# Router scaling and gate split moved to the third chunk, with the first loads cut smaller, in a two-layer streaming encoder

## The chip, the cores and the metric

The kernel runs on one core of one Trainium2 chip. The metric is the device time of one execution in microseconds (us), as the median of several runs.

## The reference, cut to what matters

Two layers over 256 tokens of width 2048. Layer 0 mixes the tokens with stick-breaking attention (16 heads), layer 1 with an mLSTM (8 heads); behind each mixer stands a mixture of 32 experts of which each token uses two.

```python
def reference(x, norm_mix, norm_ffn, norm_final, sb_w_in, sb_w_out, ml_w_in, ...):
    for i in range(DEPTH):
        h = rmsnorm(x, norm_mix[i])
        if i % N_MIXERS == 0:
            x = x + stick_breaking_mixer(h, sb_w_in[j], sb_w_out[j])   # qkv = h @ w_in: 2048 x 6144
        else:
            x = x + mlstm_mixer(h, ml_w_in[j], ml_b_i[j], ml_b_f[j], ml_g_head[j], ml_w_out[j])
        h = rmsnorm(x, norm_ffn[i])
        x = x + hierarchical_moe(h, moe_w_group[i], ..., moe_w1[i], moe_w3[i], moe_w2[i])
    return rmsnorm(x, norm_final)
```

What the change touches is the start of layer 0: `h @ w_in` for the first four heads, and the small tensors that are needed later, the router's weights (`moe_w_group`, `moe_w_expert`, 2048 x 36), its biases, the mLSTM's gate columns of `ml_w_in` (2048 x 16) and biases.

## The kernel before, in words

**Weights come in slots of 1 MB.** The projection of a layer runs in four groups of heads; a group has three chunks of 512 columns (queries, keys, values in layer 0), and a chunk four slots, each 512 rows of the weight by 512 columns. SyncE's queue loads a slot into one of three places (`raw_loaded`), ScalarE rounds it into a high part (`split_hi`, L417, semaphore `hi_made`), VectorE subtracts to get the low part (`split_lo`, L421, `lo_made`), and TensorE multiplies each of them with the high and low parts of the transposed x (`project`, 48 products of 256 columns for a slot of chunks 0 and 1, 24 of 512 for one of chunk 2). All of `lo_made`'s counts are in slot order: TensorE waits for slot j with `lo_made >= j + 1`, and the queue loads slot j once `lo_made` is j - 2. Places of both parts are three as well, so ScalarE can be at most three slots ahead of TensorE.

**The order on ScalarE and VectorE is written out.** `schedule` makes a list of steps with a position in eighths of a slot: the split of slot j stands at position 8(j - 2), the evacuation of the three chunks (`take_chunk` on VectorE, `take_values` on ScalarE) at 32, 64 and 96, just behind the split of slots 6, 10 and, for the last, 13 (slots 12 and 13 are the next group's first two). Each engine walks the list in order, and whatever it waits for holds all behind it. In the first group of layer 0, the step of chunk 0 also has these, in L1528 and L1576 to L1583 on VectorE and L1340 on ScalarE:

```python
if kind == "first" and k == 0:
    scale_router(layer)          # waits small_loaded, multiplies router_w by the norm's scale
...
if kind == "first" and k == 0:
    split_gates(act)             # waits small_loaded[0], rounds gate_w into gate_hi
```

`small_loaded[0]` counts all twenty small loads that GpSimd issues one behind the other (`load_small`, L610 to L615, then L668 to L673): six of router weights, two of biases, eight of gate columns, four more. GpSimd also splits slot 1 of each layer (`split_lo_one`, L640) before it issues them, and masks the attention scores of all groups behind them (`keep_causal`, L646).

**The start.** SyncE loads three scale rows, x in two pieces of 1 MB (128 tokens each), and slots 0, 1 and 2. TensorE turns x (`turn_x`, L713) into eight PSUM banks' worth of tiles, "units" u of two k-tiles; for each ScalarE writes the scaled high part (L1222) and VectorE the low part (L1482). Between them ScalarE splits slot 0 (behind u = 1) and slot 1 (behind u = 3), and VectorE slot 0's low part (behind u = 1). Slots 1 and 2 of `lo_made`: the low part of slot 1 comes from GpSimd, and VectorE adds that count itself behind its eight units.

After the four groups come the output projection, the router, and the experts, whose weights SyncE streams while TensorE works.

## Time and profile before

| what | before |
|---|---|
| median of 3 runs (lowest to highest) | 1791.12 us (1789.12 to 1791.99) |
| the profiled execution: its time, its span | 1790.06 us, 1788.3 us |
| busy: TensorE, VectorE, ScalarE, GpSimd | 1561.9 (87%), 728.8 (41%), 423.0 (24%), 63.2 us (4%) |
| mean granted TensorE clock | 0.944 |
| read from memory | 540.83 MB, 304 GB/s over the span |
| chain that ended last, by engine | PE 48%, issue 29%, DMA 14%, SP's queue 3%, others 2% or less each |

The page shows the busy tenths of TensorE in 40 slices of 44.7 us: `7599999999997887788699999999999887888775`. The second slice, 44.7 to 89.4 us, is the emptiest of all but the last; the granted clock has its lowest digit there as well (`9799...`).

### The profile page before, as it was taken

What the parts mean: (1) busy time and instruction counts of PE and PEld (TensorE: products, weight loads), DVE (VectorE), ACT (ScalarE), POOL (GpSimd) and SP (SyncE); (2) the same over time, 40 slices, a digit from 0 to 9 for tenths busy, and PEclk for the clock granted to TensorE, in tenths of its full rate; (3) what the DMA queues carried; (4) which work ended last, traced back from release to release, by engine and by line L of the source; (5) the groups of instructions that cost most, each with busy time, mean ns of one, the idle gap of its engine ahead of it and who ended that gap; (6) DMA issues with size and microseconds to landing.
All of it is one profiled execution on the core that took longest, in us unless ns stands there. A gap on an engine that the chain in (4) does not pass through costs nothing.

```text
span 1788.3 us, 25607 instructions
## 1 busy us (share of the span) xinstructions
PE 1561.9 (87%) x9901; PEld 1066.0 (60%) x9901; DVE 728.8 (41%) x1167; ACT 423.0 (24%) x571; POOL 63.2 (4%) x90
## 2 busy tenths in 40 slices
PE   7599999999997887788699999999999887888775
PEld 7599999888642343234267889988874332334331
DVE  4254444443432232223155657567433322232223
ACT  5143434442200000000053343333320000000002
POOL 2200001000100000000010000000000000000000
PEclk9799999999999998899799999999999988998897
DMA  7355554666999999999955454565789999999996
GB/s 262 102 166 165 164 166 162 236 233 237 360 379 427 424 425 425 428 425 424 424 211 181 149 189 164 166 217 211 267 319 392 421 425 425 427 424 425 425 427 264
DMA packets 149644, 543.79 MB, mean 304 GB/s; under 512 B 8865, under 2 KB 25681, under 8 KB 116433
## 3 DMA queue, kind: packets, MB, share of 16 engines
q1 hardware_dynamic: 148448, 541.14, 77.8%
q0 software_dynamic: 1136, 1.82, 0.5%
q8 instruction: 42, 0.69, 0.1%
q14 instruction: 18, 0.14, 0.0%
HBM read 540.83 MB, written 2.10 MB: 304 GB/s over the span
## 4 chain that ended last, share of the span: by engine, by line
PE 48%; issue 29%; DMA 14%; SPq 3%; DVE 2%; ACT 2%; POOL 1%; POOLq 1%; DVEq 0%; ACTq 0%
PE psum_G L706 26%; PE psum_S L706 14%; DMA ring<-in_moe_w 14%; PE psum_A L706 5%; SPq L521 3%; PE psum_T L706 3%; DVE w_lo L421 1%; ACT w_hi L417 1%; POOLq L642 1%; ACT h L1365 0%; POOL arena L668 0%; ACT arena L1199 0%; POOL router_w L610 0%; POOL router_w L612 0%; DVE x L1710 0%
## 5 line engine op out<-in xcount | busy, mean ns | idle before, releaser
L706 PE MATMUL psum_A<-ring,arena 128*32 128x512 f32 x2048 | 299.3, 714 | 147.1 <-DMA ring<-in_moe_w 143.1
L421 DVE TENSOR_TENSOR w_lo<-ring,w_hi 128x2048 fp32r<-128x2048 f32 x126 | 288.8, 2298 | 286.4 <-ACT w_hi L417 281.0
L417 ACT CAST w_hi<-ring 128x2048 fp32r<-128x2048 f32 x128 | 243.8, 1908 | 236.9 <-PE psum_G L706 157.4
L706 PEld LDWEIGHTS psum_A<-ring,arena 128*32 128x32 f32 x2048 | 68.8, 120 | 321.4 <-issue 319.6
L1843 DVE COPY arena_two<-psum_A 128x512 f32<-128x512 f32 x64 | 44.2, 691 | 382.6 <-PE psum_T L706 348.0
L1875 DVE TENSOR_TENSOR x<-x,psum_S 128x512 f32<-128x512 f32 x128 | 88.0, 687 | 174.9 <-PE psum_S L706 174.9
L706 PE MATMUL psum_G<-xT_hi,w_hi 128*128 128x256 f32 x512 | 148.8, 291 | 2.9 <-DVE w_lo L421 1.9
L706 PE MATMUL psum_G<-xT_hi,w_lo 128*128 128x256 f32 x512 | 144.7, 283 | 0.0
L706 PE MATMUL psum_G<-xT_lo,w_hi 128*128 128x256 f32 x512 | 144.7, 283 | 0.0
L706 PE MATMUL psum_G<-ring,arena_two 128*32 128x512 f32 x976 | 121.8, 619 | 21.7 <-DMA ring<-in_moe_w 21.6
L1381 ACT ACTIVATE arena_two<-psum_T 128x64 f32<-128x64 f32 x64 | 14.3, 223 | 480.5 <-PE psum_T L706 480.5
L706 PE MATMUL psum_S<-arena,arena_two 128*128 128x512 f32 x256 | 124.9, 617 | 0.1
L706 PE MATMUL psum_G<-arena_two,h 128*128 128x128 f32 x1024 | 122.2, 278 | 1.1 <-DVEq L1721 1.1
L706 PEld LDWEIGHTS psum_G<-arena_two,h 128*128 128x128 f32 x1024 | 116.9, 192 | 2.9 <-issue 2.9
L706 PE MATMUL psum_G<-w_hi,xT_hi 128*128 128x512 f32 x256 | 100.6, 393 | 0.0
L706 PEld LDWEIGHTS psum_T<-fold,arena_two 128*128 128x128 f32 x512 | 66.8, 204 | 56.4 <-issue 54.4
L706 PEld LDWEIGHTS psum_G<-xT_hi,w_hi 128*128 128x128 f32 x512 | 98.0, 191 | 3.6 <-DVE w_lo L421 2.2
L706 PE MATMUL psum_G<-w_lo,xT_hi 128*128 128x512 f32 x256 | 99.7, 390 | 0.0
L706 PE MATMUL psum_G<-w_hi,xT_lo 128*128 128x512 f32 x256 | 99.6, 389 | 0.0
L706 PEld LDWEIGHTS psum_G<-xT_lo,w_hi 128*128 128x128 f32 x512 | 98.0, 191 | 0.3
L706 PEld LDWEIGHTS psum_G<-xT_hi,w_lo 128*128 128x128 f32 x512 | 97.9, 191 | 0.0
L706 PE MATMUL psum_S<-xT_hi,w_hi 128*128 128x256 f32 x256 | 74.6, 291 | 21.7 <-DVE w_lo L421 21.7
(239 smaller groups left out, 2086.0 us busy)
## 6 DMA issues: line engine op xcount, KB each, us to landing
ring<-in_moe_w SPq DMA_DIRECT2D x378, 1024.0 KB, 19.5
ring<-in_sb_w_in SPq DMA_DIRECT2D x48, 1024.0 KB, 5.0
ring<-in_ml_w_in SPq DMA_DIRECT2D x48, 1024.0 KB, 5.1
ring<-in_sb_w_out SPq DMA_DIRECT2D x16, 1024.0 KB, 4.9
ring<-in_ml_w_out SPq DMA_DIRECT2D x16, 1024.0 KB, 5.1
turned_slots<-in_moe_w SPq DMA_DIRECT2D x6, 1024.0 KB, 12.3
x<-in_x SPq DMA_DIRECT2D x2, 1024.0 KB, 5.9
out_x<-h SPq DMA_DIRECT2D x4, 512.0 KB, 2.8
```

The lines of the kernel that those rows point to most:

```text
L417: act.copy(w_hi[:, slot_place(j), :], ring[:, slot_place(j), :]).then_inc(hi_made, 1)
L421: dve.tensor_tensor(w_lo[:, slot_place(j), :], ring[:, slot_place(j), :], w_hi[:, slot_place(j), :].bitcast(F32), ALU.subtract).then_inc(l ...
L521: sp_eng.dma_start(dst, src).then_inc(slot_loaded[n], 16)
L642: pool.drain().then_inc(pool_lo_made, 1)
L706: return pe.matmul(dst, lhsT, rhs, start=start, stop=stop, skip_group_check=True)
L1381: act.activation(ex, psum[t][:, 0:2 * CAP], ACT.Exp, scale=-1.0).then_inc(silu_exp, 1)
L1843: dve.tensor_copy(acc, psum[a][:, :]).then_inc(emptied[a], 1)
L1875: dve.tensor_tensor(xs, xs, psum[s][:, :], ALU.add).then_inc(emptied[s], 1)
```

## The change

It makes five edits. The first moves, in the first group of each layer, the router scaling, and in layer 0 also the thresholds and the gate split, from the step of chunk 0 (position 32) to that of chunk 2 (position 96). The second loads x in four pieces of 512 KB, by column halves, and lets TensorE turn units 0 to 3 once the first half of the columns is there. The third loads slot 0 of layer 0 in two halves of 512 KB, and splits and waits for them apart; its split now stands behind u = 3 on both engines. The fourth takes the low part of slot 1 in layer 0 from GpSimd and gives it to VectorE behind u = 5, with ScalarE's high part behind u = 4. The fifth makes GpSimd's small loads of layer 0 wait until `lo_made` is 3, that is for the low part of slot 2.

```diff
+        def first_slot_hi(act):
+            act.wait_ge(first_half_loaded, 16)
+            act.copy(first_slot(w_hi, 0), first_slot(ring, 0)).then_inc(first_half_hi, 1)
+            act.wait_ge(raw_loaded[0], 16)
+            act.copy(first_slot(w_hi, 1), first_slot(ring, 1)).then_inc(hi_made, 1)
+
+        def first_slot_lo(dve):
+            dve.wait_ge(first_half_hi, 1)
+            dve.tensor_tensor(first_slot(w_lo, 0), first_slot(ring, 0), first_slot(w_hi, 0).bitcast(F32),
+                              ALU.subtract).then_inc(first_half_lo, 1)
+            dve.wait_ge(hi_made, 1)
+            dve.tensor_tensor(first_slot(w_lo, 1), first_slot(ring, 1), first_slot(w_hi, 1).bitcast(F32),
+                              ALU.subtract).then_inc(lo_made, 1)
...
-            for b in range(TB):
-                sp_eng.dma_start(x[:, b, :], x_in[0, b * P:(b + 1) * P, :]).then_inc(x_loaded[b], 16)
+            for n in range(2):
+                for b in range(TB):
+                    c = slice(n * D // 2, (n + 1) * D // 2)
+                    sp_eng.dma_start(x[:, b, c], x_in[0, b * P:(b + 1) * P, c]).then_inc(x_loaded[n], 16)
+            for half in range(2):
+                sp_eng.dma_start(first_slot(ring, half).rearrange("p (k n) -> p k n", k=2),
+                                 sb_w_in[0].rearrange("(k p) n -> p k n", p=P)[:, 2 * half:2 * half + 2, 0:COLS]
+                                 ).then_inc(raw_loaded[0] if half else first_half_loaded, 16)
...
-            split_lo_one(0)
+            pool.wait_ge(lo_made, RAW)
             load_small(0)
...
                 for u in range(KT // 2):
+                    if layer == 0 and u % 4 == 0:
+                        pe.wait_ge(x_loaded[u // 4], 16 * TB)
...
-                    pe.wait_ge(lo_made, mix_slot(layer, i, j) + 1)
+                    if layer == 0 and isinstance(i, int) and i == 0 and j == 0:
+                        pe.wait_ge(first_half_lo, 1)
+                    else:
+                        pe.wait_ge(lo_made, mix_slot(layer, i, j) + 1)
...
+                                    if j == 0 and kk == 2:
+                                        pe.wait_ge(lo_made, 1)
...
-                    if u == 3 or (u == 1 and layer == 0):
-                        split_hi(act, layer, 0, u // 2)
+                    if layer == 0 and u == 3:
+                        first_slot_hi(act)
+                    if u == (3 if layer else 4):
+                        split_hi(act, layer, 0, 1)
...
-                    if step == "chunk" and kind == "first" and k == 0:
+                    if step == "chunk" and kind == "first" and k == 2:
                         split_gates(act)
...
-                    if u == 1 and layer == 0:
-                        split_lo(dve, layer, 0, 0)
-
-                dve.wait_ge(pool_lo_made, layer + 1)
-                dve.drain().then_inc(lo_made, 1)
+                    if layer == 0 and u == 3:
+                        first_slot_lo(dve)
+                    if layer == 0 and u == 5:
+                        split_lo(dve, layer, 0, 1)
+
+                if layer:
+                    dve.wait_ge(pool_lo_made, 1)
+                    dve.drain().then_inc(lo_made, 1)
...
-                    if kind == "first" and k == 0:
+                    if kind == "first" and k == 2:
                         scale_router(layer)
...
-                        if kind == "first" and k == 0:
+                        if kind == "first" and k == 2:
                             dve.wait_ge(consts_made, 1)
```

**VectorE, from the split of slot 6 in layer 0 on.** Before (`arena` is here the query buffer, the gate columns or the thresholds' neighbours; L1510 and L1508 take chunks 0 and 1, L1528 scales the router, L1582 splits the gates):

```order
L421 TENSOR_TENSOR w_lo<-ring,w_hi 128x2048 [waits hi_made]
L1510 SCALAR_TENSOR_TENSOR arena<-psum_G,arena 128x512 [waits filled_G0]
L1510 SCALAR_TENSOR_TENSOR arena<-psum_G,arena 128x512 [waits filled_G1]
L1528 TENSOR_TENSOR router_w<-router_w,scales 128x576 [waits small_loaded_0]
L1578 TENSOR_SCALAR thresholds<-iota 1x7 [waits consts_made]
L1582 TENSOR_TENSOR gate_lo<-arena,gate_hi 128x256 [waits gate_hi_made]
L421 TENSOR_TENSOR w_lo<-ring,w_hi 128x2048 [waits hi_made] x4
```

Now, with the changed kernel's line numbers (L424 is the split, L1563 the router's scaling, L1617 the gates):

```order
L424 TENSOR_TENSOR w_lo<-ring,w_hi 128x2048 [waits hi_made]
L1545 SCALAR_TENSOR_TENSOR arena<-psum_G,arena 128x512 [waits filled_G0]
L1545 SCALAR_TENSOR_TENSOR arena<-psum_G,arena 128x512 [waits filled_G1]
L424 TENSOR_TENSOR w_lo<-ring,w_hi 128x2048 [waits hi_made] x4
L1543 TENSOR_TENSOR arena<-psum_S,arena 128x512 [waits filled_S0]
L1543 TENSOR_TENSOR arena<-psum_S,arena 128x512 [waits filled_S1]
L424 TENSOR_TENSOR w_lo<-ring,w_hi 128x2048 [waits hi_made] x3
L1553 TENSOR_SCALAR arena<-psum_G,rstd 128x512 [waits filled_G1]
L1563 TENSOR_TENSOR router_w<-router_w,scales 128x576 [waits small_loaded_0]
L1613 TENSOR_SCALAR thresholds<-iota 1x7 [waits consts_made]
L1617 TENSOR_TENSOR gate_lo<-arena,gate_hi 128x256 [waits gate_hi_made]
```

The wait for the small loads stood ahead of the splits of slots 7 to 13 and now stands behind them; the next split behind it is slot 14's, which the loop over the later groups begins with.

**VectorE at the start.** Before, between the four units on banks T and those on A:

```order
L421 TENSOR_TENSOR w_lo<-ring,w_hi 128x2048 [waits hi_made]
L1482 SCALAR_TENSOR_TENSOR xT_lo<-psum_A,scales,xT_hi 128x256 [waits row_hi_made]
L1482 SCALAR_TENSOR_TENSOR xT_lo<-psum_A,scales,xT_hi 128x256
```

Now:

```order
L1514 SCALAR_TENSOR_TENSOR xT_lo<-psum_A,scales,xT_hi 128x256
L438 TENSOR_TENSOR w_lo<-ring,w_hi 128x1024 [waits first_half_hi]
L441 TENSOR_TENSOR w_lo<-ring,w_hi 128x1024 [waits hi_made]
L1514 SCALAR_TENSOR_TENSOR xT_lo<-psum_S,scales,xT_hi 128x256 [waits row_hi_made]
L1514 SCALAR_TENSOR_TENSOR xT_lo<-psum_S,scales,xT_hi 128x256
L1514 SCALAR_TENSOR_TENSOR xT_lo<-psum_S,scales,xT_hi 128x256 [waits row_hi_made]
L1514 SCALAR_TENSOR_TENSOR xT_lo<-psum_S,scales,xT_hi 128x256
L424 TENSOR_TENSOR w_lo<-ring,w_hi 128x2048 [waits hi_made]
L1514 SCALAR_TENSOR_TENSOR xT_lo<-psum_T,scales,xT_hi 128x256 [waits row_hi_made]
```

The first split moved from behind u = 1 to behind u = 3 and became two halves; slot 1's split came in behind u = 5.

**GpSimd.** Before, and then now, between its constants and the router's loads:

```order
L640 TENSOR_TENSOR w_lo<-ring,w_hi 128x2048 [waits hi_made]
L610 DMA router_w<-in_moe_w_group 128x6x4
L612 DMA router_w<-in_moe_w_expert 128x6x32
L610 DMA router_w<-in_moe_w_group 128x5x4
L612 DMA router_w<-in_moe_w_expert 128x5x32
```

```order
L636 DMA router_w<-in_moe_w_group 128x6x4 [waits lo_made]
L638 DMA router_w<-in_moe_w_expert 128x6x32
L636 DMA router_w<-in_moe_w_group 128x5x4
L638 DMA router_w<-in_moe_w_expert 128x5x32
```

The subtraction is gone, and the first load has the wait for `lo_made`; the order of the loads is the same.

## Rows read from the trace of the kernel before

**Rows 1.** Waits of TensorE, whole run: engine, tile, line, releaser: total us, times, longest
```profile
PE psum_A L706 <- DMA ring<-in_moe_w: 143.1, 85, 3.0
...
PE psum_S L706 <- DVE w_lo L421: 21.7, 1, 21.7
```

**Rows 2.** Windows, layer 0, first group: busy us (instructions) per engine, granted clock, DMA share, GB/s
```profile
16.70:57.75 41.05, 41.01 (x340) 40.81 (x340) 18.88 (x27) 19.03 (x32) 12.60 (x11) 1.00 0.61 189
57.75:79.40 21.65, 0.00 (x1) 0.00 (x0) 3.67 (x5) 4.57 (x4) 6.61 (x10) 0.56 0.08 6
79.40:87.55 8.15, 8.13 (x49) 8.13 (x50) 4.37 (x2) 1.24 (x1) 0.00 (x0) 0.70 0.89 312
87.55:109.40 21.85, 21.85 (x99) 18.09 (x98) 10.40 (x7) 8.36 (x6) 0.00 (x0) 1.00 0.52 172
```

**Rows 3.** Timeline of VectorE: start us, duration us, line, operation, count, idle before, releaser
```profile
44.71 1.28 DVE L1510 SCALAR_TENSOR_TENSOR arena<-psum_G,arena 128x512 f32<-128x512 f32 x2
...
74.83 0.76 DVE L1528 TENSOR_TENSOR router_w<-router_w,scales 128x576 f32<-128x576 f32 x1 [28.84 <-DMA gate_b<-in_ml_b_f]
```

**Rows 4.** Timeline of GpSimd, 23 to 74 us: its loads for layer 0
```profile
23.02 1.02 POOL L610 DMA_DIRECT2D router_w<-in_moe_w_group  x1 [0.67 <-issue]
...
52.82 0.75 POOL L668 DMA_DIRECT2D arena<-in_ml_w_in  x1 [2.83 <-issue]
...
70.90 0.76 POOL L668 DMA_DIRECT2D arena<-in_ml_w_in  x1 [1.89 <-issue]
...
73.24 0.52 POOL L673 DMA_DIRECT2D gate_b<-in_ml_b_f  x1
```

**Rows 5.** Timeline of GpSimd, the six router loads for layer 1, first and last
```profile
456.05 0.88 POOL L610 DMA_DIRECT2D router_w<-in_moe_w_group  x1 [86.16 <-DVEq L1785]
...
486.06 0.87 POOL L612 DMA_DIRECT2D router_w<-in_moe_w_expert  x1 [5.63 <-issue]
```

**Rows 6.** Windows during the loads of rows 4 (two stretches) and of rows 5
```profile
20.00:50.00 30.00, 30.00 (x252) 30.00 (x252) 15.72 (x20) 15.73 (x25) 8.79 (x9) 1.00 0.73 234
50.00:72.00 22.00, 7.75 (x65) 7.55 (x63) 0.00 (x0) 0.00 (x0) 6.37 (x9) 0.74 0.10 7
456.00:487.00 31.00, 28.81 (x250) 17.49 (x249) 12.30 (x39) 3.98 (x10) 5.29 (x7) 1.00 0.92 350
```

**Rows 7.** Landing: x's two loads (issued 2.21, 2.66 us), first three slots (from 3.14)
```profile
DMA to landing us min/median/max: 4.9/5.9/6.9
...
DMA to landing us min/median/max: 9.0/11.1/12.7
```

**Rows 8.** Timelines of the start: TensorE, ScalarE, VectorE
```profile
9.75 1.94 PE L713 MATMUL psum_T<-ident,x 128*128 128x128 f32 x8 [5.97 <-DMA x<-in_x]
...
16.74 0.39 PE L706 MATMUL psum_G<-xT_hi,w_hi 128*128 128x256 f32 x1 [1.93 <-DVE w_lo L421]
...
10.94 1.63 ACT L1222 ACTIVATE xT_hi<-psum_T,scales 128x256 fp32r<-128x256 f32 x4 [8.84 <-PE psum_T L713]
...
12.46 1.90 ACT L417 CAST w_hi<-ring 128x2048 fp32r<-128x2048 f32 x1
...
14.39 2.29 DVE L421 TENSOR_TENSOR w_lo<-ring,w_hi 128x2048 fp32r<-128x2048 f32 x1 [0.84 <-ACT w_hi L417]
...
18.39 1.66 DVE L1482 SCALAR_TENSOR_TENSOR xT_lo<-psum_S,scales,xT_hi 128x256 fp32r<-128x256 f32 x4
...
22.55 2.29 DVE L421 TENSOR_TENSOR w_lo<-ring,w_hi 128x2048 fp32r<-128x2048 f32 x1 [0.94 <-POOLq L642]
```

**Rows 9.** Timelines at the start of group 1: ScalarE, GpSimd, TensorE
```profile
109.37 1.91 ACT L417 CAST w_hi<-ring 128x2048 fp32r<-128x2048 f32 x1 [1.97 <-PE psum_G L706]
...
116.00 0.41 POOL L646 TENSOR_SCALAR_AFFINE_SELECT arena_three<-arena_three 128x256 f32<-128x256 f32 x1 [42.24 <-DVEq L1589]
...
120.53 1.04 PE L706 MATMUL psum_A<-arena_three,arena 128*128 128x256 f32 x6
```

**Rows 10.** Timeline of VectorE in layer 1, first split of group 1
```profile
999.39 2.29 DVE L421 TENSOR_TENSOR w_lo<-ring,w_hi 128x2048 fp32r<-128x2048 f32 x1 [3.67 <-ACT w_hi L417]
```

More of the change, by code:

```diff
@@ L304, in build @@
         row_ready = sem("row_ready")
-        x_loaded = [sem(f"x_loaded_{b}") for b in range(TB)]
+        x_loaded = [sem(f"x_loaded_{n}") for n in range(2)]
+        first_half_loaded = sem("first_half_loaded")
+        first_half_hi = sem("first_half_hi")
+        first_half_lo = sem("first_half_lo")
         last_scale_loaded = sem("last_scale_loaded")
@@ L421, in split_lo, with first_slot @@
             dve.tensor_tensor(w_lo[:, slot_place(j), :], ring[:, slot_place(j), :], w_hi[:, slot_place(j), :].bitcast(F32),
+                              ALU.subtract).then_inc(lo_made, 1)
+        def first_slot(tensor, half):
+            return tensor[:, slot_place(0), half * (SLOT // 2):(half + 1) * (SLOT // 2)]
+        def first_slot_hi(act):
[9 more added lines that the diff above has]
+            dve.tensor_tensor(first_slot(w_lo, 1), first_slot(ring, 1), first_slot(w_hi, 1).bitcast(F32),
                               ALU.subtract).then_inc(lo_made, 1)
@@ L581, in _ @@
                                  ).then_inc(rows_loaded, 16)
-            for b in range(TB):
-                sp_eng.dma_start(x[:, b, :], x_in[0, b * P:(b + 1) * P, :]).then_inc(x_loaded[b], 16)
+            for n in range(2):
[6 more added lines that the diff above has]
+                                 ).then_inc(raw_loaded[0] if half else first_half_loaded, 16)
             for layer in (0, 1):
                 if layer == 0:
-                    mix_stream(layer, 0, range(RAW))
+                    mix_stream(layer, 0, range(1, RAW))
                 mix_stream(layer, 0, range(RAW, 12))
@@ L1182, in _ @@
                     pe.wait_ge(x_final, 1)
-                else:
-                    for b in range(TB):
-                        pe.wait_ge(x_loaded[b], 16)
                 turn_x(layer)
```

## The prediction

> **What bounds the kernel now.** I read the page's slices first, then TensorE's waits, then windows over the first group of layer 0, then each engine's timeline there. Over the whole run TensorE waits in two places of any size: 143.1 us in 85 pieces for expert weights, none over 3.0 us, and one single piece of 21.7 us for a low part of a weight slot [rows 1]. The first is the weight stream of the expert stages, which this change does not touch. The second is its subject. The windows place it: seven slots run without a gap from 16.70 to 57.75 us (41.01 of 41.05 us busy, 5.86 us a slot), then TensorE does nothing until 79.40, and slot 7 behind it takes 8.15 us at a mean granted clock of 0.70 [rows 2], since the clock had fallen to its lower level (1.2 of 2.4 GHz) in the idle time. VectorE's timeline says why: it takes chunk 0 at 44.71, then waits 28.84 us for the landing of `gate_b`, and scales the router at 74.83 [rows 3]. Slot 7's split stands behind that, on VectorE and on ScalarE alike. The landing is the last of GpSimd's twenty small loads, issued one after another from 23.02 to 73.24 us [rows 4]. So the first 80 us are bound by a chain of small loads whose data nobody needs until the router and layer 1.
>
> **1. The wait moves from chunk 0 to chunk 2.** What goes: the idle 21.65 us and the surplus of slot 7, 8.15 - 5.86 = 2.3 us [rows 2]. Together 23.9 us. Splits 7 to 13 and the evacuation of chunk 1 now stand ahead of the wait, so TensorE can run through the end of chunk 2 whatever the small loads do. What is late next is the landing itself, as seen from the new place; that needs two times, T (the last small load has landed) and E (TensorE has ended chunk 2).
>
> E: chunk 2 ended at 109.40 before [rows 2]. Less 23.9 and less the 2.1 us of point 2 it ends at 83.4.
>
> How long after E may T be? Before, in group 1, ScalarE began slot 14's high part at 109.37; over VectorE's low part, the clipping, exponential and logarithm of the first score, GpSimd's mask ended at 116.00 + 0.41, about 116.5 with its drain, and TensorE used it at 120.53 [rows 9]. That is 4.0 us of slack. With the wait in front, ScalarE first rounds the gate columns (a quarter-size copy, which I put at 0.5 us), so T may be 3.5 us behind E: **the bound is T = 86.9**. GpSimd's masks are also queued behind its loads, but it has issued the last one 1.6 us ahead of T (73.24 against 74.83), and so is no later than the others. The router's scaling (0.76 us [rows 3]) and two small steps run on VectorE while ScalarE still casts slot 14; nothing for them.
>
> T: GpSimd's first load now waits for the third low part. By point 2 that is there at 24.3, and 0.7 for the first issue (the idle of row 23.02) makes 25.0 against 23.02. From there to the first gate load (52.82) it took 29.8 us before for six router and two bias loads, 5.0 for each router load with the biases counted in, under a DMA share of 0.73 [rows 4, 6]; the stream of slots is the same now, so 54.8. The eight gate loads are what changes cover: before, seven spacings of (70.90 - 52.82)/7 = 2.58 us, but with the weight stream asleep (share 0.10) [rows 4, 6]. Now slots flow. Bounds: 2.58 us below, and 6.0 above, the spacing of the router loads for layer 1, (486.06 - 456.05)/5, under a nearly full stream (share 0.92) [rows 5, 6]. In chunks 1 and 2 the share is about 0.5 to 0.6 [rows 2], one transfer of some 2.7 us in each 5.5 to 5.9. A gate load that falls between two transfers should pay 2.6 and one that meets a transfer about 3.2 us, so two fit into a slot's time: I take 3.3 us, nearer the idle row because half the time there is no transfer to meet. T = 54.8 + 7 x 3.3 + 3.9 (from 70.90 to 74.83) = **81.8, 5 us ahead of the bound. No new stall.** The bounds give T = 76.8 and 100.7; the point at which it costs is a spacing of (86.9 - 54.8 - 3.9)/7 = 4.0 us.
>
> **2. The start.** Before: x's second piece lands at about 9.6 (2.66 + 6.9 [rows 7]), TensorE turns from 9.75, ScalarE begins at 10.94 (1.19 behind), VectorE's low part of slot 0 runs 14.39 to 16.68, TensorE starts at 16.74, slot 1's low part is counted when VectorE is free at 22.55 [rows 8]. Now the first 1 MB that lands is the left half of both token blocks, at 2.21 + 4.9 = 7.1 [rows 7], so turning starts at 7.3 and ScalarE at 8.5. Four units at 0.75 (half of 1.5, 10.94 to 12.46) end at 11.5. The first half of slot 0 lands at about 10.8 (slot 0 whole at 12.1, 3.14 + 9.0, less half a MB), so its cast, 1.0 us (half of 1.90), ends at 12.5 and the second half's at 13.5. VectorE starts 0.95 behind ScalarE, does four units in 3.3 us (1.66 for two [rows 8]) until 12.8, the half in 1.2 (half of 2.29 and a little) until 14.0: TensorE starts at 14.05, not 16.74. The second half's low part is ready at 15.2, and TensorE wants it after 12 products, at 15.5. Slot 1: landed at 14.6, cast until 16.6, u = 5 until 17.3; VectorE does u = 5 until 18.1 and slot 1 until 20.4, where TensorE wants it at 14.05 + 5.86 = 19.9. So half a us is lost again and slot 1 starts at 20.4 instead of 22.55: **2.1 us**. Slot 2's low part is ready at 20.4 + 1.6 + 2.3 = 24.3, wanted at 26.3. Bounds: nothing, if halves land no sooner, and 2.7, TensorE's whole head start. SyncE issues three loads more at about 0.45 us each (two for x, one for slot 0), still ahead of the transfers, which take 1.3 us a piece; nothing.
>
> **3. Layer 1.** VectorE's scaling moves from position 32 to 96 there too; its data are long loaded. It now stands in front of the first split of group 1, where VectorE idles 3.67 us [rows 10], so its 0.9 us are covered. The place it leaves was followed by an idle wait for the gate products; no gain.
>
> **4. Passing through.** The later stages start from TensorE's progress, the expert stream too, so what is gained here moves everything behind it earlier.
>
> **Sum.** 23.9 + 2.1 = 26.0 us. The profiled execution took 1790.06 us (span 1788.3 and 1.8 around it), which gives 1764.1; the median of the runs is 1.1 above it, so 1765.1.
>
> **Two rules weighed.** First landings: the load spacing rose from 2.58 to 5.0 and 6.0 us as the share rose from 0.10 to 0.73 and 0.92. The Trainium skill (DMA: Bandwidth & Descriptors, Queues, rings and completion order) says that each DMA engine alternates between queues packet by packet, and that a completion lands only after all earlier writes of that engine across its queues; by that rule every load that meets a slot's transfer waits for it, which is rival B. Second, issuing: GpSimd's first load was issued in 1.02 us though VectorE's split started at 22.55, half a us before it, and lasted to 24.84, and later ones took 0.87 [rows 4, 5, 8]. The Trainium skill (SBUF — State Buffer, SBUF: two separate sides) warns that GpSimd can be locked out of writing descriptors while VectorE holds the port they share. By that rule the change would pay up to one split of 2.3 us for a load, as VectorE is now busy when the gate loads run; the row shows 0.15 us.
>
> **Rivals.** A, *the start gives nothing*: the halves land as late as the whole, or VectorE, which took over slot 1, is the bound; 1767. For it: VectorE's work there is packed without a gap in my reckoning. Against: x's first load lands 2.5 us before its second.
> B, *the stall moves to group 1*: gate loads at 5.0 us, as the router's were in the same stream. T = 54.8 + 35 + 3.9 = 93.7, 6.8 us past the bound, 1772. For it: chunk 0's stream is the nearest row in kind. Against: part of that spacing belongs to the larger transfers of the router's weights, and to doubled slots behind the row of norms.
> C, *slower than before*: every one of the fourteen paced loads costs 6.5 us, the last spacing of rows 5 (5.63 idle and 0.87). T = 25.0 + 6 x 6.5 + 4 + 7 x 6.5 + 3.9 = 117.4; the stall is 30.5 us and 2.3 for the clock, 33 against 26 gained: 1798. It decides from about 6.0 us a load on. Against: it needs the share of the expert stage, 0.92, where the projection has half.
> D, *the change doesn't do what it says*: some other wait stops the splits at chunk 0; 1788. The order of VectorE's rows speaks against it.
>
> **How the numbers follow.** Forecast 0.55, A 0.12, B 0.27 (anywhere between 1767 and 1775), C 0.03, D 0.03. The range takes in the forecast's own bounds (1762 to 1767), A, and most of B: 1762 to 1773.5. This kernel's runs can tell 0.2% (3.6 us) from no change. Faster by more: the forecast, A, B, 0.95 with a rest; within: 0.02; slower: 0.03.
>
> **What would show it.** Right: no wait of TensorE over 1 us between 20 and 110; clock 1.00 there; TensorE's first product near 14.1, the end of chunk 2 near 83; the router's scaling near 82 to 84, right behind the evacuation. Wrong: a wait in group 1 for `softplus_masked` or a low part, with the last small load past 87; gate loads 4 us apart or more; the first product later than 15.

## The result, and the profile after

| | before | changed |
|---|---|---|
| median (lowest to highest) | 1790.98 us (1789.12 to 1791.99) | 1774.68 us (1774.45 to 1775.27) |
| span of the profiled execution | 1788.3 us | 1772.9 us |
| mean granted clock | 0.944 | 0.948 |

The ratio is 0.9911, with a 95% interval of 0.9894 to 0.9928: faster by 16.3 us, where 26.0 were forecast, and 1.2 us above the top of the range. The time lies in the stretch that the prediction gave to rival B.

The lines of the profile's page on TensorE and GpSimd (busy tenths of TensorE in 40 slices, its granted clock in tenths, busy tenths of GpSimd):

```profile
PE   7989999999997888788699999999999787788775
...
PEclk9999999999998998899799999999999988998897
...
POOL 1120100100100000000011000000000000000000
```

TensorE's waits, longest in total first (engine, tile, line, releaser: us, times, longest); in the changed kernel's numbering L732 is the matmul helper, L674 GpSimd's drain behind a mask, and `ring<-in_moe_w` an expert's weights:

```profile
engine line waited for: us in total, times, longest us
PE psum_A L732 <- DMA ring<-in_moe_w: 147.2, 82, 3.3
PE psum_G L732 <- DMA ring<-in_moe_w: 16.7, 9, 5.2
PE psum_A L732 <- POOLq L674: 6.5, 1, 6.5
```

The one piece of 21.7 us [rows 1] is gone, and a new one of 6.5 us stands in its place: TensorE waits for GpSimd's mask. The waits for expert weights (147.2 and 16.7) are those of before within a few us (143.1, and 21.6 on the other bank). Windows over the first group, over the new wait, and over what follows it (start and end, length, busy us and instructions of TensorE, its weight loads, VectorE, ScalarE and GpSimd, then granted clock, DMA share, GB/s):

```profile
14.70:84.80 70.10, 68.86 (x486) 64.90 (x487) 37.87 (x34) 33.98 (x40) 11.70 (x15) 1.00 0.67 219
96.10:102.60 6.50, 0.04 (x2) 0.02 (x1) 4.07 (x5) 2.31 (x4) 0.40 (x1) 0.77 0.31 90
102.60:110.00 7.40, 7.40 (x44) 7.17 (x45) 3.94 (x3) 5.18 (x6) 2.44 (x3) 0.74 0.32 101
```

The group runs from 14.70 to 84.80 us at full clock with 1.2 us of idle time; no slot waits for a low part as slot 7 did [rows 2]. The clock falls in the wait and is at 0.74 of full speed on average over the 7.4 us behind it, that is partly at its lower level, 1.2 of 2.4 GHz. The chain that holds the mask, on GpSimd's timeline (first router load, first and last gate load, last small load, first mask):

```profile
25.98 1.01 POOL L636 DMA_DIRECT2D router_w<-in_moe_w_group  x1 [21.66 <-DVE w_lo L424]
...
57.52 0.75 POOL L694 DMA_DIRECT2D arena<-in_ml_w_in  x1 [5.83 <-issue]
...
89.36 0.76 POOL L694 DMA_DIRECT2D arena<-in_ml_w_in  x1 [4.65 <-issue]
...
91.70 0.52 POOL L699 DMA_DIRECT2D gate_b<-in_ml_b_f  x1
...
101.64 0.40 POOL L672 TENSOR_SCALAR_AFFINE_SELECT arena_three<-arena_three 128x256 f32<-128x256 f32 x1 [9.43 <-DVEq L1624]
```

and on VectorE's (evacuation of chunk 2, then the router's scaling behind the wait):

```profile
84.80 0.75 DVE L1553 TENSOR_SCALAR arena<-psum_G,rstd 128x512 f32<-128x512 f32 x1 [1.15 <-PE psum_G L732]
...
94.71 0.76 DVE L1563 TENSOR_TENSOR router_w<-router_w,scales 128x576 f32<-128x576 f32 x1 [9.16 <-DMA gate_b<-in_ml_b_f]
```

Against [rows 4]: the chain begins 3.0 us later, takes 31.5 us instead of 29.8 to the first gate load, and then (89.36 - 57.52)/7 = 4.55 us from one gate load to the next instead of 2.58. The issues follow the landings, about 0.3 us behind; the eight gate loads took from issue to landing

```profile
DMA to landing us min/median/max: 2.2/4.3/5.2
```

which is 4.3 us in the middle and 2.2 for the shortest. The trace's records of single packets show what the others wait for. The load issued at 78.42 has a slot's transfer beside it, 528 packets from 79.41 to 83.15 on SyncE's queue (q1; GpSimd's is q0). From its issue to 82.50, and then from 82.50 to 83.20 (packets, MB, share of the engines):

```profile
q1 hardware_dynamic: 458, 0.94, 74.6%
...
q1 hardware_dynamic: 70, 0.11, 41.8%
q0 software_dynamic: 32, 0.02, 7.9%
```

All 32 packets of the small load run behind the first 458 of the slot's. Of the seven spacings, six have more than half of a slot's transfer in front of the small load's packets and are 4.02 to 5.54 us; the seventh (from the load at 66.44, whose packets ran before the next transfer began) is 2.54. The last small load has landed at 94.7 (T), 9.9 us behind the end of chunk 2 (E, 84.8). The mask begins 6.9 us after T, at 101.64, and TensorE goes on with

```profile
102.59 2.08 PE L732 MATMUL psum_A<-arena_three,arena 128*128 128x256 f32 x6 [6.46 <-POOLq L674]
```

By the prediction's bound a stall is as long as T is past E + 3.5: 94.7 - (84.8 + 3.5) = 6.4 us, and the trace has 6.46.

The start, on TensorE, ScalarE, VectorE and TensorE again:

```profile
8.06 1.97 PE L739 MATMUL psum_T<-ident,x 128*128 128x128 f32 x8 [4.27 <-DMA x<-in_x]
...
14.74 0.39 PE L732 MATMUL psum_G<-xT_hi,w_hi 128*128 128x256 f32 x1 [1.63 <-DVE w_lo L438]
...
9.29 1.63 ACT L1252 ACTIVATE xT_hi<-psum_T,scales 128x256 fp32r<-128x256 f32 x4 [7.18 <-PE psum_T L739]
...
16.16 1.90 ACT L420 CAST w_hi<-ring 128x2048 fp32r<-128x2048 f32 x1 [0.81 <-DMA ring<-in_sb_w_in]
...
17.97 0.83 ACT L1252 ACTIVATE xT_hi<-psum_S,scales 128x256 fp32r<-128x256 f32 x2
...
18.83 0.88 DVE L1514 SCALAR_TENSOR_TENSOR xT_lo<-psum_S,scales,xT_hi 128x256 fp32r<-128x256 f32 x2 [2.17 <-ACT xT_hi L1252]
...
19.62 2.28 DVE L424 TENSOR_TENSOR w_lo<-ring,w_hi 128x2048 fp32r<-128x2048 f32 x1
...
21.96 0.39 PE L732 MATMUL psum_G<-xT_hi,w_hi 128*128 128x256 f32 x1 [1.20 <-DVE w_lo L424]
```

TensorE's first product comes 2.0 us earlier than in [rows 8] (14.74 against 16.74), but slot 1's products begin at 21.96, where they began at 22.59 before: 0.6 us is what is left of the head start.

### The profile page after: what moved, and what is told of

The parts are those of the page before. It is cut to its first block, busy times and chain, and to the rows that moved or that the text cites. A ratio compares the mean times of both kernels' runs of the same rounds, so it can differ in the third digit from the quotient of the medians.

```text
span 1772.9 us, 25611 instructions
## 1 busy us (share of the span) xinstructions
PE 1563.9 (88%) x9901; PEld 1071.3 (60%) x9901; DVE 731.8 (41%) x1169; ACT 423.8 (24%) x572; POOL 60.2 (3%) x89
## 4 chain that ended last, share of the span: by engine, by line
PE 50%; issue 30%; DMA 13%; SPq 3%; DVE 2%; ACT 1%; POOL 1%; POOLq 0%; DVEq 0%; ACTq 0%
PE psum_G L732 26%; PE psum_S L732 15%; DMA ring<-in_moe_w 12%; PE psum_A L732 5%; PE psum_T L732 3%; SPq L541 2%; DVE w_lo L424 1%; ACT w_hi L420 1%; DMA ring<-in_sb_w_in 1%; POOL arena L694 0%; ACT arena L1229 0%; POOL router_w L636 0%; POOL router_w L638 0%; POOLq L668 0%; DVE x L1745 0%
## 5 line engine op out<-in xcount | busy, mean ns | idle before, releaser
L732 PE MATMUL psum_A<-ring,arena 128*32 128x512 f32 x2048 | 296.8, 710 | 150.9 <-DMA ring<-in_moe_w 147.2
L424 DVE TENSOR_TENSOR w_lo<-ring,w_hi 128x2048 fp32r<-128x2048 f32 x126 | 289.1, 2298 | 286.3 <-ACT w_hi L420 281.8
L732 PEld LDWEIGHTS psum_A<-ring,arena 128*32 128x32 f32 x2048 | 68.6, 120 | 322.2 <-issue 320.7
L732 PE MATMUL psum_G<-xT_hi,w_hi 128*128 128x256 f32 x512 | 149.4, 292 | 3.1 <-DVE w_lo L438 1.6
L732 PE MATMUL psum_G<-xT_hi,w_lo 128*128 128x256 f32 x512 | 145.1, 283 | 0.0
L732 PE MATMUL psum_G<-xT_lo,w_hi 128*128 128x256 f32 x512 | 145.1, 283 | 0.0
L732 PE MATMUL psum_G<-ring,arena_two 128*32 128x512 f32 x976 | 120.8, 615 | 16.8 <-DMA ring<-in_moe_w 16.7
L732 PE MATMUL psum_G<-arena_two,h 128*128 128x128 f32 x1024 | 125.3, 282 | 1.1 <-DVEq L1756 1.1
L732 PE MATMUL psum_S<-arena,arena_two 128*128 128x512 f32 x256 | 124.9, 617 | 0.1
L732 PEld LDWEIGHTS psum_G<-arena_two,h 128*128 128x128 f32 x1024 | 120.1, 196 | 2.9 <-issue 2.9
L732 PEld LDWEIGHTS psum_T<-fold,arena_two 128*128 128x128 f32 x512 | 68.1, 207 | 57.2 <-issue 55.3
L732 PEld LDWEIGHTS psum_G<-xT_hi,w_hi 128*128 128x128 f32 x512 | 98.6, 192 | 4.1 <-DVE w_lo L438 1.9
L732 PE MATMUL psum_G<-w_hi,xT_hi 128*128 128x512 f32 x256 | 100.6, 393 | 0.0
L732 PE MATMUL psum_G<-w_lo,xT_hi 128*128 128x512 f32 x256 | 99.7, 390 | 0.0
L732 PE MATMUL psum_G<-w_hi,xT_lo 128*128 128x512 f32 x256 | 99.6, 389 | 0.0
L732 PEld LDWEIGHTS psum_G<-xT_lo,w_hi 128*128 128x128 f32 x512 | 98.5, 192 | 0.3
L732 PEld LDWEIGHTS psum_G<-xT_hi,w_lo 128*128 128x128 f32 x512 | 98.4, 192 | 0.0
L732 PEld LDWEIGHTS psum_S<-arena,arena_two 128*128 128x128 f32 x256 | 41.2, 188 | 84.2 <-issue 48.8
```

Source lines behind the costliest of these rows:

```text
L424: dve.tensor_tensor(w_lo[:, slot_place(j), :], ring[:, slot_place(j), :], w_hi[:, slot_place(j), :].bitcast(F32), ALU.subtract).then_inc(l ...
L732: return pe.matmul(dst, lhsT, rhs, start=start, stop=stop, skip_group_check=True)
```

## The experiments

All times are medians; the kernel before, run beside them, had 1791.6 (e1 to e4), 1790.7 (e5 to e7) and 1791.0 us (e8 to e10). The kernels of e1 to e4 and e7 to e10 compute the same as the kernel before; e5 and e6 leave a part out. T is when the last small load has landed, E when VectorE begins to take the last of chunk 2.

**e1, the first edit alone.**

```diff
 (kernel before)
-if kind == "first" and k == 0:   scale_router, thresholds, gate_lo; split_gates
+if kind == "first" and k == 2:
```

> The kernel before with the first edit alone (router scaling, thresholds and gate split at chunk 2 instead of chunk 0); x in two pieces, slot 1's low part on GpSimd, small loads from 23 us. Theory (the wait has moved, and the spacing of the small loads under the weight stream decides): chunk 2 ends at 109.4 - 23.9 = 85.5; the chain of loads is as long as in the changed kernel, 94.7 - 26.0 = 68.7 us, and ends at 91.7, 2.7 us past the bound of 3.5 us behind chunk 2, so a stall of about 3 us in group 1 and about 1769 to 1770, faster than the whole change. Rival (the stall in group 1 has to do with the new start, VectorE taking slot 1): no stall here and 1766.

Measured: 1768.58 us, ratio 0.987 (0.9853 to 0.9886), 6 us faster than the whole change. The wait for the mask:

```profile
PE psum_A L706 <- POOLq L648: 0.8, 1, 0.8
```

and VectorE's evacuation and scaling:

```profile
85.28 0.75 DVE L1518 TENSOR_SCALAR arena<-psum_G,rstd 128x512 f32<-128x512 f32 x1 [1.15 <-PE psum_G L706]
...
89.55 0.76 DVE L1528 TENSOR_TENSOR router_w<-router_w,scales 128x576 f32<-128x576 f32 x1 [3.53 <-DMA gate_b<-in_ml_b_f]
```

T is 89.5 and E 85.28, so the stall by the bound is 0.7 us; 0.8 are there. The chain, from the first issue to T, was 66.5 us long here, 2.2 less than in the changed kernel and than the theory had it, so a stall of 0.8 stands where 3 were expected. The one edit gains 23.0 us; with the four others it is 16.3.

**e2, the start and the hold without the move.**

```diff
 (changed kernel)
-if kind == "first" and k == 2:
+if kind == "first" and k == 0:   at all three places
```

> The changed kernel with the move undone (scaling and split back at chunk 0), new start and hold kept. Theory: TensorE's end of stall is set by the landing of the last small load, and the hold shifts that by the 3 us by which the first load is later (25.98 against 23.02): about 1793, slower than the kernel before, and nothing of the earlier first product is seen. Rival (the start is worth its own 0.6 us whatever the loads do): 1789 to 1790.

Measured: 1793.19 us over 10 runs, ratio 1.0009 (0.9999 to 1.0018). The interval takes in no change, but the sign and the size are as expected, and the trace has the stall grown from 21.7 to 24.1 us:

```profile
PE psum_S L732 <- DVE w_lo L424: 24.1, 1, 24.1
```

The router is scaled at 77.09 instead of 74.83, and chunk 2 ends at 111.3 instead of 109.4. What the earlier first product won is gone in the same wait. With the stream asleep again, (73.10 - 55.06)/7 = 2.58 us lie between its gate loads, as in the kernel before: start and hold don't change the spacing.

**e3, no hold.**

```diff
 (changed kernel, GpSimd)
-            pool.wait_ge(lo_made, RAW)
             load_small(0)
```

> The changed kernel without the wait for lo_made ahead of the small loads, so that they begin at about 4.5 us, in the same queue as x and the first slots. Theory (chain length decides): the chain ends near 94.7 - 21.5 = 73, before chunk 2 ends at 84.8, no stall in group 1, 8.5 us gained against the change: about 1766, at most 1 us more if the loads delay x and slots 0 to 2. Rival (the hold was needed: the small loads slow the start by several us): 1768 to 1772 with the first product later than 16.

Measured: 1766.98 us, ratio 0.9862 (0.9845 to 0.9878). No stall in group 1, the scaling is right behind the evacuation:

```profile
87.58 0.75 DVE L1552 TENSOR_SCALAR arena<-psum_G,rstd 128x512 f32<-128x512 f32 x1 [1.15 <-PE psum_G L731]
...
88.24 0.75 DVE L1562 TENSOR_TENSOR router_w<-router_w,scales 128x576 f32<-128x576 f32 x1
```

but E is 2.8 us later than in the changed kernel. The small loads now move beside x and the first slots, and ScalarE waits for slot 0 and, 1.3 us at 17.45 instead of 0.8 at 16.16, for slot 1:

```profile
13.06 1.05 ACT L432 CAST w_hi<-ring 128x1024 fp32r<-128x1024 f32 x1 [0.43 <-DMA ring<-in_sb_w_in]
...
17.45 1.90 ACT L420 CAST w_hi<-ring 128x2048 fp32r<-128x2048 f32 x1 [1.30 <-DMA ring<-in_sb_w_in]
```

Slot 1's products begin at 23.25 instead of 21.96, which is 1.3 of the 2.8 us. The rest is clock, which fell behind TensorE's longer wait for that slot (1.8 us instead of 1.2), while in the changed kernel it stayed at 1.00:

```profile
23.20:26.00 2.80, 2.75 (x17) 2.75 (x18) 2.80 (x5) 2.60 (x8) 0.69 (x1) 0.72 0.47 136
26.00:28.00 2.00, 2.00 (x12) 2.00 (x12) 0.96 (x1) 1.80 (x7) 0.00 (x0) 0.54 0.97 367
```

So both readings hold a part: the hold does protect the start, by 2.8 us, and costs 6.5 us of stall and 2 of clock at the other end. By the first `o_lo` of group 1 (VectorE's low part of an attention output, a row behind the masks; 112.66 against 118.37) that leaves 5.7 us for e3; the medians are 7.7 apart. The first product (15.42) moved less than the rival had it.

**e4, the small loads waited for at the output projection.**

```diff
 (changed kernel, layer 0 alone)
-if kind == "first" and k == 2:
+if kind == "out" and k == 0:     scale_router, thresholds, gate_lo; split_gates
```

> The changed kernel with layer 0's scaling, thresholds and gate split at the first chunk of the output projection, some 250 us later, hold and start kept. Theory (only the wait in front of group 1 costs): no stall of TensorE between 22 and 300 us, landing still at about 94.7, and 8.5 us less than the change (6.5 of stall and 2.0 of lower clock): about 1766. Rival (GpSimd's own place in the loads holds the masks of group 1, since it stands behind the same queue): a wait for the mask of some us stays, 1768 to 1773.

Measured: 1768.12 us (1766.99 to 1769.08), ratio 0.9869 (0.9853 to 0.9885). TensorE's waits up to 320 us:

```profile
PE psum_T L739 <- DMA x<-in_x: 4.1, 1, 4.1
PE psum_S L1211 <- DMA arena<-in_ml_g_head: 3.5, 1, 3.5
PE psum_G L732 <- DVE w_lo L424: 1.1, 1, 1.1
PE psum_G L732 <- issue: 0.9, 1, 0.9
```

Behind these come only pieces of 0.2 us. The 6.5 us are not there, though GpSimd's last load is issued at 91.84, as late as in the changed kernel. GpSimd's own place costs 0.2 us (its first mask is at 92.35). By the trace the stall and its clock are worth 8.0 us: VectorE's first `o_lo` of group 1 comes at 110.33 instead of 118.37, with E the same (84.78). The medians differ by 6.6. The expert stage of layer 0 was 1.7 us longer in e4's profile (464.8 from ScalarE's first row of the norm ahead of the experts, at 426.34, to VectorE's first unit of layer 1, at 891.12; in the changed kernel's 463.1, from 433.85 to 896.97). In the twelve profiles that stage lies between 463.1 and 464.8 with no order in the kernels, so I read it as spread.

**e5 and e6, what slows the small loads.** e5 thins the weight stream and leaves VectorE's splits: of slots 3 to 11 it loads 16 of 512 columns, so a slot is 32 KB instead of 1 MB and the projection is left out in part. e6 thins the splits and leaves the stream: VectorE makes 64 of 2048 columns of the same slots' low parts, and leaves out the rest.

```diff
 (changed kernel; e5, SyncE, slots 3 to 11 of layer 0's first group)
+                    if layer == 0 and isinstance(i, int) and i == 0 and j >= RAW:
+                        dst, src = dst[:, :, 0:16], src[:, :, 0:16]
 (e6, VectorE, the same slots)
+            c = slice(0, 64) if layer == 0 and isinstance(i, int) and i == 0 and RAW <= j < 12 else slice(0, SLOT)
```

> The changed kernel in which slots 3 to 11 of layer 0's first group load only 16 of 512 columns of each row (the rest of a slot keeps what it held, so the projection is left out in part); VectorE and ScalarE split whole slots as before. Theory (the small loads are slow because they meet the transfers of slots): from about 30 us the spacing falls to 2.6 us for gate columns, as in the kernel before's idle stretch, against 4.55 in the changed kernel, the chain ends near 75 to 78 and the stall in group 1 is gone. Rival (GpSimd is kept from writing descriptors while VectorE's splits hold the port they share): the spacing stays at 4 us and more, since the splits are all there.

> The changed kernel in which VectorE makes the low part of slots 3 to 11 of layer 0's first group for 64 of 2048 columns only (left out for the rest); the slots' transfers are whole. Theory (transfers): the spacing of the gate loads stays between 4 and 5 us and the chain ends past 90. Rival (port): the spacing falls towards 2.6 us, the chain ends near 78.

Measured, first and last gate load of e5 (and the one ahead of the last, where whole slots are loaded again), then of e6:

```profile
47.22 0.75 POOL L696 DMA_DIRECT2D arena<-in_ml_w_in  x1 [2.98 <-issue]
...
63.12 0.75 POOL L696 DMA_DIRECT2D arena<-in_ml_w_in  x1 [1.91 <-issue]
...
66.98 0.76 POOL L696 DMA_DIRECT2D arena<-in_ml_w_in  x1 [3.11 <-issue]
```

```profile
55.03 0.76 POOL L695 DMA_DIRECT2D arena<-in_ml_w_in  x1 [4.79 <-issue]
...
84.14 0.76 POOL L695 DMA_DIRECT2D arena<-in_ml_w_in  x1 [4.28 <-issue]
```

Without the stream the spacing is (66.98 - 47.22)/7 = 2.82 us, and 2.65 up to 63.12. Without the splits it is (84.14 - 55.03)/7 = 4.16. Six other runs with both (e1, e3, e4, e7, e9, e10) have 4.36 to 4.71. It is the stream: without it nearly all of the 2 us are gone, without the splits 0.2 to 0.6, hardly more than the spread among like runs, and the length of an issue (0.75 us) is the same in all of them. In e5 the load issued at 63.12 is the one that has a whole slot's transfer in front of it again, and it alone costs 3.86 us. The router's loads shorten too: from the first issue (25.77) to the first gate load it is 21.5 us, against 31.5 in the changed kernel. Both kernels ran once, at 1767.1 and 1768.2 us; e5 has no stall, e6 one of 1.6, where the bound gives 90.1 - (85.08 + 3.5) = 1.5.

**e7, x in two pieces again.**

```diff
 (changed kernel)
-            for n in range(2):
-                for b in range(TB):
-                    c = slice(n * D // 2, (n + 1) * D // 2)
-                    ...then_inc(x_loaded[n], 16)
+            for b in range(TB):
+                sp_eng.dma_start(x[:, b, :], x_in[0, b * P:(b + 1) * P, :]).then_inc(x_loaded[0], 16)
```

> The changed kernel with x in two pieces of 1 MB again, turning begins with both; slot 0 stays in halves. Theory (cutting x in four won TensorE only part of what was forecast because the pieces of 4 KB rows go slower and slots 0 and 1 land later): the first product is about 1 us later than 14.74 but slot 1 lands earlier than 16.1, and slot 1's products begin at 21.5 to 22.5; end of chunk 2 within 0.5 us of 84.8, time within 0.7 us of 1774.7. Rival (the cut of x is worth its 1.7 us of earlier turning): everything up to chunk 2 is 1.5 us later; but the landing of the small loads, then also later, sets the time: about 1776.

Measured: 1776.05 us (1774.77 to 1777.57). The first product is at 16.45, 1.7 us later, but E at 85.36, 0.6 later. The stall:

```profile
PE psum_A L730 <- POOLq L672: 6.7, 1, 6.7
```

Of the 1.4 us to the changed kernel T has 0.8 (95.5 against 94.7), so the time does not tell the two readings apart. E, 0.6 later, is nearer to the theory's 0.5 than to the rival's 1.5, and the landings agree with the theory: slot 1 was issued at 4.53 and landed at 15.0, against 5.74 and 16.1 in the changed kernel.

**e8, the gate columns on SyncE's queue.**

```diff
 (changed kernel)
+                    mix_stream(layer, 0, range(RAW, RAW + 1))
+                    ... the eight loads of gate_w, on sp_eng, .then_inc(gates_loaded, 16)
+                    mix_stream(layer, 0, range(RAW + 1, 12))
```

> The changed kernel with the eight gate-column loads on SyncE's queue, right behind slot 3, with a semaphore of their own; GpSimd keeps the other twelve. Everything else, the wait at chunk 2 too, as in the change. Theory (the length of GpSimd's chain is the whole cause): GpSimd's last load lands near 26 + 31.5 + 4 = 62, far ahead of chunk 2, no stall in group 1, 1766 to 1768. Rival (short rows of 32 bytes in the slots' own queue delay slots 4 and 5): a wait of TensorE for a low part between 25 and 50 us, chunk 2 ends 2 us or more later than 84.8.

Measured: 1766.83 us (1764.65 to 1767.00), ratio 0.9862 (0.9845 to 0.9878). GpSimd's first and last load, VectorE's evacuation and scaling:

```profile
26.50 1.01 POOL L643 DMA_DIRECT2D router_w<-in_moe_w_group  x1 [22.18 <-DVE w_lo L425]
...
64.31 0.52 POOL L702 DMA_DIRECT2D gate_b<-in_ml_b_f  x1
...
85.33 0.75 DVE L1556 TENSOR_SCALAR arena<-psum_G,rstd 128x512 f32<-128x512 f32 x1 [1.15 <-PE psum_G L735]
...
86.00 0.75 DVE L1566 TENSOR_TENSOR router_w<-router_w,scales 128x576 f32<-128x576 f32 x1
```

The wait at chunk 2 is still there and costs nothing, since the last of GpSimd's loads is issued at 64.3. Chunk 2 ends 0.5 us later than in the changed kernel, as its first product (15.20) does; TensorE waits for no low part between 25 us and E. The length of the chain was the cause: with the wait where it was, 7.9 us came back, and by E and the first `o_lo` (110.42 instead of 118.37) as much.

**e9, slot 1 behind unit 5; e10, the old start with the wait at the output projection.**

```diff
 (e9: e4's kernel, ScalarE)
-                    if u == (3 if layer else 4):
+                    if u == (3 if layer else 5):
                         split_hi(act, layer, 0, 1)
 (e10: kernel before, layer 0 alone)
-if kind == "first" and k == 0:
+if kind == "out" and k == 0:
```

> The kernel of the run at the output projection (no stall), with ScalarE's high part of slot 1 behind unit 5 instead of unit 4. Theory (the start lost 1.5 us because ScalarE waited 0.81 us for slot 1's landing with unit 5 queued behind it, and VectorE 2.17 us for unit 5): slot 1's products begin near 20.5 instead of 21.96, chunk 2 ends near 83.5 instead of 84.8, time about 1.2 us below the run at the output projection (1768.1), 1767. Rival (VectorE is the bound of the start in any order): no difference in chunk 2's end over 0.3 us.

> The kernel before with layer 0's scaling, thresholds and gate split at the output projection alone; old start, GpSimd on slot 1, small loads from 23 us. Theory (the new start is worth 0.5 us): chunk 2 ends at 85.3, no stall, time about 0.5 us above the run at the output projection, 1768.5. Rival (the new start is worth its 2 us of earlier first product): 1770.

Measured: e9 1766.43 us (1765.09 to 1767.63), e10 1767.24 us (1766.63 to 1769.19), e4 had 1768.12. VectorE in e9 does units 4 and 5 in one piece, with no wait between them, and TensorE no longer waits for slot 1:

```profile
16.48 1.65 DVE L1514 SCALAR_TENSOR_TENSOR xT_lo<-psum_S,scales,xT_hi 128x256 fp32r<-128x256 f32 x4
...
83.95 0.75 DVE L1553 TENSOR_SCALAR arena<-psum_G,rstd 128x512 f32<-128x512 f32 x1 [1.15 <-PE psum_G L732]
```

E is 83.95, 0.8 us earlier than e4's although x and slot 0 landed later in this run and the first product is at 15.33; from the first product to E it is 68.6 us instead of 70.0 (e4: 14.79 to 84.78). The theory's 1.3 us at E came out as 0.8. In e10 that distance is 68.6 as well:

```profile
17.01 0.39 PE L706 MATMUL psum_G<-xT_hi,w_hi 128*128 128x256 f32 x1 [1.72 <-DVE w_lo L421]
...
85.61 0.75 DVE L1518 TENSOR_SCALAR arena<-psum_G,rstd 128x512 f32<-128x512 f32 x1 [1.16 <-PE psum_G L706]
```

with the first product at 17.01. So the new start in its order is worth 0.8 us (85.61 against 84.78), near the 0.5 of e10's theory and not the rival's 2, and with slot 1 behind unit 5 it is worth 1.7. The medians don't show these differences: e10's is 0.9 below e4's, where 0.5 above was expected.

One thing bears on e1. Up to E, e10 and e1 are the same program, and yet e10's last small load is issued at 87.20 and e1's at 84.53. From the first issue to the last the chain took 61.6 us in e1, 63.9 in e10, 60.2 in e9, 65.9 in e4 and 65.7 in the changed kernel. How the loads fall between the slots' transfers moves it by several us, so e1's stall of 0.8 us could as well have been 3.

## Why the prediction was wrong

Point 1, what goes: right. The 21.65 us of idle time and the 2.3 us of lower clock behind it are gone; e1 has E at 85.28, where the step gives 109.4 - 23.9 = 85.5.

Point 1, **the bound (T may be 3.5 us behind E)**: right. Four kernels with a stall measure it: 6.46 us against 6.4 by the bound, 0.8 against 0.7 (e1), 1.6 against 1.5 (e6), 6.7 against 6.6 (e7).

Point 1, **T = 81.8: this step failed**. Measured 94.7. Of the 12.9 us, 1.0 come from the first issue (25.98 for 25.0), 1.7 from the router's part (31.5 us for 29.8), 8.7 from the seven spacings (4.55 us for 3.3) and 1.4 from the tail (5.35 us for 3.9), which also ran under the stream now. The term that decided was the spacing. The prediction had the deciding point at 4.0 us between bounds of 2.6 and 6.0, and chose 3.3 by reckoning that a load that meets a transfer pays about 3.2 us and that two fit into a slot's time. Both were wrong. In the changed kernel a load that met a transfer cost 4.0 to 5.5 us, because its packets ran late in the transfer or at its end, and six of seven met one. The packet records say why so many: a slot's packets run for 3.6 to 3.8 us of every 5.4 to 5.8, not for 2.7, which leaves a gap of about 2 us; from the end of one load's packets to the start of the next one's it takes 2.1 us even with the stream asleep (in the kernel before, 54.77 to 56.89). The row that was nearest in kind, 5.0 us for router loads in the same stream [rows 4], was set aside for their size; e5 and e6 show that the stream accounts for nearly all of the difference between 2.6 and 4.55. Rival B, priced at T = 93.7, a stall of 6.8 and 1772 us, is what happened. It left out the clock: it fell in the 6.5 us of idle time, and the first products behind ran at 0.74 on average, which is 2.0 us more (from E to the first `o_lo` it takes 33.57 us instead of the 25.09 of e8, which has no stall: 8.5 more, of which 6.46 are the wait). The start, too, gave 1.5 us less than B had with the rest of the sum (point 2).

Point 2, **the start, 2.1 us: 0.6 measured.** Two terms were mis-sized. x's left half landed for TensorE at 8.06 instead of 7.3, and slot 1 at 16.1 instead of 14.6, so that ScalarE idled 0.81 us with unit 5 behind the wait, and VectorE 2.17 us for unit 5. The prediction took the landings from transfers in large pieces, and put SyncE's three extra issues at nothing. Slot 1 was issued at 5.74, where it was 3.6 before, and landed at 16.1 instead of 14.7; in e7, with x in two pieces and so two issues fewer, it was 4.53 and 15.0. Whether the smaller pieces or the later issue made it late is not separated by the runs. e9 gets 0.8 of it back by the order alone.

Point 3, layer 1: no new wait of TensorE between 890 and 1320 us, as forecast. Point 4, passing through: right. Where the norm ahead of layer 0's experts begins, the changed kernel is 16.3 us ahead (433.85 against 450.13), and the median is 16.3 us lower; e4 is 23.8 ahead there and 23.5 in the median.

The sum with measured terms: 23.9 + 0.6 - 6.46 - 2.0 = 16.0 us.

Of the two rules weighed, the first has the outcome: a load that met a transfer waited for it. The Trainium skill (DMA: Bandwidth & Descriptors, Queues, rings and completion order) has the engines alternate packet by packet, and a completion wait for earlier writes of its engine on any queue. The second half was not what took the time here: the small load's data themselves start late (82.53 for the load issued at 78.42, against 1.5 us behind the issue with the stream asleep), and its first completion is written 0.04 us behind the first of them. Why the data wait so long, no run tells.

The second rule, by its own wording, does not reach this kernel. The Trainium skill (SBUF — State Buffer, SBUF: two separate sides) ties the lock on descriptor writing to VectorE operations in a 2-port mode, and has an operation with two inputs in SBUF hold the shared pair only against GpSimd operations that read SBUF; the splits are of this second kind. The lock would have shown as a fall to 2.6 us in e6; the run shows 4.16, so the splits have 0.6 us at most. The 0.15 us that the prediction read as the split's share are not its doing either: the first load's issue also takes 1.01 us in the changed kernel, at 25.98, when VectorE's split has ended (25.67).

## What to carry to other kernels

When a wait is moved behind work that used to stand still, the thing waited for no longer runs alone: price its remaining steps by the rows taken under the load that will now be there, and ask how far the deciding value is from that row. A chain of many small loads that one engine issues one by one costs its count times a spacing, and the spacing here went from 2.58 to 4.55 us beside a weight stream; move its consumer to where the data is first needed, or put part of it on another queue, before moving its start. And a head start is worth only what the next buffer's landing lets through.

## What the runs showed that was not expected

A 16 KB load beside a 1 MB transfer did not share with it: its packets ran when more than half of the transfer's had gone, in most cases nearly all. The hold cost more than it protected: without it the first slots land later, the clock falls once and E is 2.8 us later (e3); with it the last small load is issued 19.4 us later (91.70 against 72.27), and the stall and its clock cost 8.5. Eight loads of 32-byte rows in the slots' own queue, right behind slot 3, cost TensorE no wait in the first group (e8), while on GpSimd's queue they took 32 us from the first issue to the last (57.52 to 89.36). The first edit alone, one number at three places, was faster (1768.6 us) than all five together (1774.7), and the fastest kernel of the study (e9, 1766.4 us; e8, 0.4 above it, and e3, 0.6, can't be told from it) differs from the changed one in where the wait stands and in one unit of order.
